# RWKV chunk loop of a four-layer encoder: right side in opposite rows, solve beside the state output on four blocks, 32x32 completion between 64x64 products

## The chip, the cores and the metric

The kernel runs on one core of one Trainium2 chip. The metric is the device time of one execution in microseconds. Three executions of the kernel before took 1472.31, 1472.85 and 1475.32 us (median 1472.85).

## The reference, cut to what matters

The model is an encoder of four layers on one sequence of 512 tokens of width 1024, all in float32: an RWKV-7 mixer, windowed attention, an mLSTM mixer, and a second RWKV-7 mixer. The change touches the two RWKV-7 mixers. In the reference their core is a scan over tokens with a 64x64 state for each of 16 heads:

```python
def step(S, inp):
    r_t, w_t, k_t, v_t, kk_t, b_t = inp
    sa = jnp.einsum('bhvk,bhk->bhv', S, -kk_t)
    S = S * w_t[:, :, None, :] + sa[..., None] * b_t[:, :, None, :] + v_t[..., None] * k_t[:, :, None, :]
    return S, jnp.einsum('bhvk,bhk->bhv', S, r_t)
```

The kernel works in 8 chunks of 64 tokens. Inside a chunk the values `sa` of all tokens depend on each other through a strictly triangular 64x64 matrix A for each head, so that they come from a triangular solve: `sa = -(I + A)^-1 * right side`. The inverse is put together from 32x32 parts: both diagonal 32x32 blocks are inverted for all chunks and heads at once before the loop, and the off-diagonal block is the product inverse * A-block * inverse with a minus sign. That last step is called the completion here.

## The kernel before, in words

The program is written by hand: each engine has its own instruction list, and semaphores (`wait_ge`, `then_inc`) order them. `rw_mix` is one RWKV layer up to the heads' outputs. Its projections fill TensorE with 128x128 by 512 products; then comes the chunk loop over `c` in 0..7. The 16 heads are kept as 8 pairs `p`, the even head of a pair in partitions 0 to 63 (`LO`), the odd one in 64 to 127 (`HI`). All matrices of a head are 64x64, so that a product of one head fills one of the four 64x64 blocks of the array. Which block is set by the rows where the operands lie and by the rows of the bank that it writes.

All products of the layer but the projections go through `mm` at line 848, so that the profile shows them under L848; the transposes of B and K are L959. A float32 product appears as two MATMUL and two LDWEIGHTS records; a transpose as one.

TensorE's list in chunk c, in order:

1. `complete_and_begin(c)`: 16 products for the completion (lower left part of the inverse, out to banks 2 and 3), and between them 16 products that begin the right side (A_k * V, out to banks 4 and 5). The completion products use LO->LO and HI->HI, the others the two crossed blocks.
2. `right_side_state(c)`: 16 products KK * S, added in banks 4 and 5, on LO->LO and HI->HI.
3. `turn_values(c+1)`: 16 products with 128 rows and 64 columns, to banks 0 and 1.
4. `products_r(c+1)`: 32 products on all four blocks, to banks 2 and 3.
5. `solve(c)`: 16 products, completed inverse times right side, on LO->LO and HI->HI, to banks 6 and 7.
6. `x(c+1)`: 16 products of 64x64, A times the placed 32x32 inverses, to banks 0 and 1.
7. `outputs(c)`: 16 products S * L (the state's output), then for each half of the pairs 8 products with 128 rows for the output and 8 with 128 rows for the state.
8. `turn_bk(c+1)`: 8 transposes of 128x128, to banks 0 and 1.

ScalarE (ACT) in chunk c: `read_rhs` (L599, two), `values(c+1)` (L592 and L593, two each), `read_sa` (L606, four), `read_y` (L612, two), `keep_bkt(c+1)` (L557 to L559, six), and `place_inverse(c+2)` (L581, four copies that put the 32x32 inverses into a zeroed 64x64 tile, 128 columns wide with its transpose). VectorE (DVE): `mask_r(c+1)` (L679, two), `mask_x(c+1)` (L746, two), `advance(c)` (L758 and L762), `complete_u(c+1)` (L752, two), `place_transpose(c+2)` (L732, four). GpSimd squares the outputs (L512) beside them. SyncE's list has two things in the loop: the reload of h after chunk 3, and the next weights, which wait for the last `us_ready`, since the placed inverses lie in the weights' slots.

What the change touches: the constants at lines 360 to 380, the views `tu`, `xs`, `us`, `x_bank` (419 to 445), SyncE's wait (488), GpSimd's memset (507), `place_inverse` (571, with its calls 628 to 642), `place_transpose`, `mask_x`, `complete_u` (724 to 753), VectorE's loop (829 to 844), and TensorE's functions from line 914 to 1083.

Of the kernel before, what the change touches and what calls it, by code (L numbers as in the profile page):

```python
# [9 lines left out]
ALU = mybir.AluOpType  # L10
# [3 lines left out]
P = 128  # L14
T = 512
D = 1024
KT = D // P
NT = T // P
C = 64
# [343 lines left out]
A_US = A_XS + 512  # L363
A_S = A_US + 512
# [15 lines left out]
SIDES = ((0, LO), (1, HI))  # L380

# [10 lines left out]
def rw_mix(m, prm, w2a2, reset_src, n0, spill):  # L392
# [29 lines left out]
    gmask, xmask = m.view(A_CONST + C_GMASK, P), m.view(A_CONST + C_XMASK, C)  # L422
# [6 lines left out]
    tu = [m.view(m.slot(n0 + 29 + c), KT, P) for c in range(NC)]  # L429
    z = [m.view(A_Z + 1024 * (c % 2), NH, C) for c in range(NC)]  # L430
    xs, us = m.view(A_XS, KT, C), m.view(A_US, KT, C)
# [4 lines left out]
    quarter = lambda bank: bank[:, 0:256].rearrange("p (k c) -> p k c", c=C)  # L436
    blocks = lambda bank: bank[:, :].rearrange("p (k c) -> p k c", c=P)
# [11 lines left out]
    for j in range(KT):  # L449
# [16 lines left out]
    gathered, step, t_turned, tu_cleared, t_placed, u_placed = (m.sem(n) for n in (  # L466
        "gathered", "inverse_step", "t_turned", "tu_cleared", "t_placed", "u_placed"))
# [7 lines left out]
    with nc.Block() as block:  # L475
        @block.sync
        def _(sp):
# [10 lines left out]
            sp.wait_ge(us_ready.handle, us_ready.at(2 * NC))  # L488
# [4 lines left out]
        def _(pool):  # L493
# [10 lines left out]
            for c in range(BC):  # L504

                pool.wait_ge(tile_done.handle, tile_done.at(place["g", BC + c] + 1))
                nc.gpsimd.memset(tu[c], 0.0).then_inc(tu_cleared.handle, 1)
# [7 lines left out]
        def _(act):  # L515
# [55 lines left out]
            def place_inverse(c):  # L571

                if c == 0:
                    act.wait_ge(t_turned.handle, t_turned.at(1))
                if c < BC:
                    act.wait_ge(tu_cleared.handle, tu_cleared.at(c + 1))
                else:
                    act.wait_ge(us_ready.handle, us_ready.at(2 * (c - BC + 1)))
                for g in range(4):
                    rows, at = slice(Q * g, Q * g + Q), Q * (g % 2)  # L580
                    last = nc.scalar.activation(tu[c][rows, :, at:at + Q],  # L581
                                                tt[rows, c // BC, :, KT * (c % BC):KT * (c % BC) + KT]
                                                .rearrange("p c n -> p n c"), ACT.Copy)
                last.then_inc(t_placed.handle, 1)

# [42 lines left out]
            place_inverse(0)  # L628
# [3 lines left out]
            place_inverse(1)  # L632
            for c in range(NC):
# [7 lines left out]
                if c + 2 < NC:  # L641
                    place_inverse(c + 2)

        @block.vector
        def _(dve):
# [78 lines left out]
            def place_transpose(c):  # L724

                if c < BC:
                    dve.wait_ge(tu_cleared.handle, tu_cleared.at(c + 1))
                else:
# [1529 lines left out]
```

## Time and profile before

| | |
|---|---|
| median of three executions | 1472.85 us |
| the profiled execution | 1473.26 us |
| its span in the trace | 1471.2 us |
| mean granted TensorE clock over the span | 0.98 of full |
| TensorE busy (matrix products) | 1356.5 us, 92% |
| VectorE busy | 719.3 us, 49% |
| ScalarE busy | 440.6 us, 30% |
| records under L848 | 6720, 187.6 us |

The span is the time from the first to the last instruction of the one profiled execution; the 2.1 us between it and the time of that execution lie around it. Busy times of TensorE are the union of its overlapping records: a stretch can be full of records and yet pass few of them, so that counts and start times say more than the busy share. In the timelines of the trace a row merges neighbouring instructions of one line and engine; its first number is the start in us from the span's start, the second the time covered, `x192` the number of records, and the bracket is the idle time ahead of the row and what ended it.

### The profile page before, as it was taken

To read this page: it belongs to the slowest core of one execution; us is meant where nothing else is said; L and a number is where in the kernel's file an instruction comes from. 1 tells how busy PE (TensorE), PEld (TensorE's weight loads), DVE (VectorE), ACT (ScalarE), POOL (GpSimd) and SP (SyncE) were. 2 spreads that over 40 slices of the span, in tenths; PEclk is the share of its full clock that TensorE was granted. 3 is DMA by queue.
4 is the path that set the end of the run, shared out by engine and by line. 5 is a ranking of instruction groups with operands and counts; after the bars stand their busy time and mean duration, and the time that the engine had idled before them with its cause. 6 is when DMAs were issued, how large, how long until landed. Compare 5 with 4: busy or idle time off the path is not lost. (4 is left out here: it accounts for less than half of the span.)

```text
span 1471.2 us, 23885 instructions
## 1 busy us (share of the span) xinstructions
PE 1356.5 (92%) x10291; PEld 713.6 (49%) x10291; DVE 719.3 (49%) x1388; ACT 440.6 (30%) x964; POOL 90.7 (6%) x82
## 2 busy tenths in 40 slices
PE   5999999988798999889899989898999999988897
PEld 3444444487544444464444446544444444478633
DVE  5784656855643002261344023434684755955552
ACT  1114243277401011460112052501114253177501
POOL 0000240100000000000000000000000241000000
PEclk9999999999999999999999989998999999999989
DMA  6222222001400222101222221113222222101211
GB/s 208 72 72 56 61 70 62 25 4 61 176 0 1 73 84 72 58 2 57 74 71 72 72 56 29 57 57 113 80 72 57 72 59 69 32 4 61 75 58 57
DMA packets 111184, 92.47 MB, mean 63 GB/s; under 512 B 5020, under 2 KB 99524, under 8 KB 110568
## 3 DMA queue, kind: packets, MB, share of 16 engines
q1 hardware_dynamic: 110376, 88.81, 19.9%
q8 instruction: 82, 1.34, 0.4%
q10 hardware_dynamic: 704, 2.13, 0.4%
q14 instruction: 22, 0.18, 0.0%
HBM read 84.64 MB, written 6.29 MB: 62 GB/s over the span
## 5 line engine op out<-in xcount | busy, mean ns | idle before, releaser
L893 PE MATMUL bank<-arena 128*128 128x512 f32 x960 | 420.1, 594 | 1.5 <-ACT arena L541 1.5
L893 PEld LDWEIGHTS bank<-arena 128*128 128x128 f32 x960 | 180.6, 190 | 224.9 <-issue 219.1
L848 PE MATMUL bank<-arena 64*64 64x64 f32 (+2 forms) x6720 | 187.6, 225 | 29.8 <-ACT arena L599 8.9
L848 PEld LDWEIGHTS bank<-arena 64*64 64x64 f32 (+1 forms) x6720 | 164.5, 135 | 66.0 <-issue 37.5
L1215 PE MATMUL bank<-arena 128*128 128x512 f32 x256 | 116.9, 618 | 4.7 <-DVE arena L1180 4.7
L159 ACT ACTIVATE arena<-arena 128x1024 f32<-128x1024 f32 x20 | 21.1, 1055 | 244.6 <-DVE arena L1186 133.4
L1215 PEld LDWEIGHTS bank<-arena 128*128 128x128 f32 x256 | 50.2, 198 | 71.8 <-issue 64.7
L1679 PE MATMUL bank<-arena 128*128 128x512 f32 x160 | 71.0, 605 | 1.6 <-PEq L301 1.6
L653 DVE SCALAR_TENSOR_TENSOR arena<-arena 128x512 f32<-128x512 f32 x96 | 72.2, 802 | 0.0
L495 POOL MEMSET arena<- 128x8 f32 x2 | 0.2, 113 | 932.9 <-DVE arena L808 932.9
L1311 PE MATMUL bank<-arena 128*128 128x512 f32 x128 | 55.2, 593 | 1.6 <-PEq L1124 1.6
L2088 PE MATMUL bank<-arena 128*128 128x512 f32 x128 | 55.8, 593 | 0.9 <-DVE arena L2132 0.9
L310 PE MATMUL bank<-arena 128*128 128x512 f32 x128 | 55.2, 593 | 1.0 <-PEq L1427 1.0
L565 ACT ACTIVATE arena<-arena 32x256 f32<-32x256 f32 x64 | 41.4, 647 | 47.0 <-DVE arena L673 46.5
L1342 PE MATMUL bank<-arena 128*128 128x512 f32 x128 | 55.2, 591 | 0.0
L1660 PE MATMUL bank<-arena 128*128 128x512 f32 x128 | 55.1, 592 | 0.0
L786 DVE RECIPROCAL arena<-arena 128x512 f32<-128x512 f32 x16 | 53.6, 3352 | 0.5
L541 ACT ACTIVATE arena<-bank 128x512 f32<-128x512 f32 x32 | 19.0, 595 | 115.1 <-PE bank L893 115.1
L1679 PEld LDWEIGHTS bank<-arena 128*128 128x128 f32 x160 | 30.8, 194 | 41.5 <-issue 41.5
L539 ACT ACTIVATE arena<-bank 128x512 f32<-128x512 f32 x16 | 9.6, 597 | 122.6 <-PE bank L893 75.2
L1876 PE MATMUL bank<-arena 128*128 128x512 f32 x96 | 42.9, 592 | 0.0
L1392 DVE TENSOR_TENSOR arena<-arena 128x160 f32<-128x160 f32 x16 | 4.1, 320 | 78.9 <-ACT arena L1369 78.7
(233 smaller groups left out, 1652.3 us busy)
## 6 DMA issues: line engine op xcount, KB each, us to landing
arena<-in_rw_w_in SPq DMA_DIRECT2D x66, 512.0 KB, 4.1
arena<-in_ml_w_in SPq DMA_DIRECT2D x24, 512.0 KB, 3.8
arena<-in_sw_w_in SPq DMA_DIRECT2D x20, 512.0 KB, 3.7
arena<-in_rw_w_out SPq DMA_DIRECT2D x16, 512.0 KB, 7.1
spill<-arena SPq DMA_DIRECT2D x2, 2048.0 KB, 8.4
arena<-spill SPq DMA_DIRECT2D x2, 2048.0 KB, 8.5
arena<-in_sw_w_out SPq DMA_DIRECT2D x8, 512.0 KB, 3.7
arena<-in_ml_w_out SPq DMA_DIRECT2D x8, 512.0 KB, 3.7
```

The costliest lines, as they stand in the source:

```text
L310: return nc.tensor.matmul(m.bank[2 * a + half][:, :], Y[:, k, a * P:(a + 1) * P], slot[:, k % 2, :], start=k == 0, stop=k == KT - 1)
L653: nc.vector.scalar_tensor_tensor(out=mix_at[g][:, k, :], in0=dx[:, k, :], scalar=col(mu_at[g], k), in1=xt[:, k, 1:T + 1], op0=ALU.mult, op ...
L786: link(nc.vector.reciprocal(rt, rt))
L848: mm = lambda out, a, b, start=True, stop=True: nc.tensor.matmul(out, a, b, start=start, stop=stop, skip_group_check=True)
L893: last = nc.tensor.matmul(bank[:, :], slot[:, k, :], mix_at[what][:, k, :], start=k == 0, stop=k == KT - 1)
L1215: return nc.tensor.matmul(nc_out[:, :], Y[:, k, a * P:(a + 1) * P], W[:, k, 512 * half:512 * half + 512], start=k == 0, stop=k == KT - 1)
L1311: last = nc.tensor.matmul(m.bank[n][:, :], xt[:, k, 1 + (n // 2) * P:1 + (n // 2 + 1) * P], slot[:, 512 * (n % 2):512 * (n % 2) + 512], st ...
L1342: last = nc.tensor.matmul(m.bank[4 + j % 4][:, :], slot[:, k, :], xt[:, k, 1:T + 1], start=k == 0, stop=k == KT - 1)
L1660: last = nc.tensor.matmul(tile_bank(n + i)[:, :], xt[:, c, 1 + (i // 2) * P:1 + (i // 2 + 1) * P], slot[:, 512 * (i % 2):512 * (i % 2) + 5 ...
L1679: last = nc.tensor.matmul(bank[:, :], slot[:, c, :], xt[:, c, 1:T + 1], start=c == 0, stop=c == KT - 1)
L1876: last = nc.tensor.matmul(z_bank(i)[:, :], m.view(m.slot(n0 + i), KT, P)[:, c, :], xt[:, c, 1:T + 1], start=c == 0, stop=c == KT - 1)
L2088: return nc.tensor.matmul(out_bank(a, half)[:, :], Y[:, k, a * P:(a + 1) * P], slot[:, k % 2, :], start=k == 0, stop=k == KT - 1)
```

## The change

The completion's products become 32x32 with the needed rows and columns alone. `x(c, p)` multiplies the off-diagonal 32x32 block of A with the inverse where that lies after the inversion (`tt`, a moving operand whose neighbouring elements are 32 apart), from rows 0:32 and 64:96 (`EARLIER`) to rows 32:64 and 96:128 (`LATER`) of bank 2. `xu(c, p)` multiplies that with `uu`, from the rows `LATER` to the rows `EARLIER` of the other half of bank 3. The copies of `place_inverse` go; `place_transpose` writes 64x64 tiles `u[c]` with the two heads' rows exchanged, and `complete_u` writes the missing 32x32 part into them with a factor of -1. The right side is formed in the opposite rows: `begun` takes LO->LO and HI->HI, KK * S and the solve take the crossed blocks. Between the products of `right_side_state(c)` stand those of `x(c + 1, p)`; between the products that begin the right side those of `xu(c, p)`; between the products of the solve those of the state's output. `products_r(c + 1)` moves behind the solve. All waits follow. Constants, semaphore names and the addresses of S and rhs change with it.

```diff
+EARLIER, LATER = (slice(0, 32), slice(64, 96)), (slice(32, 64), slice(96, 128))
+CROSSED = ((LO, HI), (HI, LO))
...
-    tu = [m.view(m.slot(n0 + 29 + c), KT, P) for c in range(NC)]
+    u = [m.view(m.slot(n0 + 29 + c // 2) + KT * C * (c % 2), KT, C) for c in range(NC)]
+    of_chunk = lambda inv, c, p: inv[:, c // BC, :, KT * (c % BC) + p]
...
-    x_bank = lambda c, g: m.bank[g if c else 2 + g]
+    x_bank, xu_bank = m.bank[2], m.bank[3]
...
-            sp.wait_ge(us_ready.handle, us_ready.at(2 * NC))
+            sp.wait_ge(sa_done.handle, sa_done.at(2 * NC))
             m.load_weights(sp, n0 + 33 + SLOTS)
...
-                if c + 2 < NC:
-                    place_inverse(c + 2)
...
 def place_transpose(c):
-                if c < BC:
-                    dve.wait_ge(tu_cleared.handle, tu_cleared.at(c + 1))
-                else:
-                    dve.wait_ge(us_ready.handle, us_ready.at(2 * (c - BC + 1)))
+                dve.wait_ge(u_cleared.handle, u_cleared.at(c // 2 + 1))
                 for g in range(4):
-                    rows, at = slice(Q * g, Q * g + Q), C + Q * (g % 2)
-                    last = nc.vector.tensor_copy(tu[c][rows, :, at:at + Q],
-                                                 uu[rows, c // BC, :, KT * (c % BC):KT * (c % BC) + KT]
+                    rows, to, at = slice(Q * g, Q * g + Q), slice(Q * (g ^ 2), Q * (g ^ 2) + Q), Q * (g % 2)
+                    last = nc.vector.tensor_copy(u[c][to, :, at:at + Q], uu[rows, c // BC, :, KT * (c % BC):KT * (c % BC) + KT]
...
-            def mask_x(c):
-                for g in range(2):
-                    dve.wait_ge(x_done.handle, x_done.at(2 * c + g + 1))
-                    nc.vector.tensor_tensor(xs[:, pairs[g], :], quarter(x_bank(c, g)), wide(xmask, 4), ALU.mult)\
-                        .then_inc(xs_ready.handle, 1)
+            def keep_x(c):
+                dve.wait_ge(x_done.handle, x_done.at(c + 1))
+                for rows in LATER:
+                    last = nc.vector.tensor_copy(xs[rows], small(x_bank)[rows])
+                last.then_inc(xs_ready.handle, 1)
 
             def complete_u(c):
-                for g in range(2):
-                    dve.wait_ge(xu_done.handle, xu_done.at(2 * c + g + 1))
-                    nc.vector.tensor_tensor(us[:, pairs[g], :], tu[c][:, pairs[g], C:P], quarter(m.bank[2 + g]), ALU.subtract)\
-                        .then_inc(us_ready.handle, 1)
+                dve.wait_ge(xu_done.handle, xu_done.at(c + 1))
+                for rows in EARLIER:
+                    last = nc.vector.tensor_scalar(u[c][rows, :, Q:C], small(xu_bank)[rows], -1.0, None, ALU.mult)
+                last.then_inc(us_ready.handle, 1)
...
             for c in range(NC):
                 if c + 1 < NC:
+                    keep_x(c + 1)
+                    place_transpose(c + 1)
                     mask_r(c + 1)
-                    mask_x(c + 1)
                 advance(c)
                 if c + 1 < NC:
                     complete_u(c + 1)
-                if c + 2 < NC:
-                    place_transpose(c + 2)
...
+            def x_begin(c):
+                if c == 0:
+                    pe.wait_ge(ga_evac.handle, ga_evac.at(2 * NC))
+                    pe.wait_ge(t_turned.handle, t_turned.at(1))
+                else:
+                    pe.wait_ge(gr_evac.handle, gr_evac.at(2 * given["r"]))
+                given["x"] = c + 1
+
+            def x(c, p):
+                for par in range(2):
+                    last = mm(x_bank[LATER[par], Q * p:Q * p + Q], ga[c][EARLIER[par], 2 * p + par, Q:C],
+                              of_chunk(tt, c, p)[EARLIER[par]])
...
+            def xu(c, p):
+                for par in range(2):
+                    last = mm(xu_bank[EARLIER[1 - par], Q * p:Q * p + Q], xs[LATER[par], p, :], of_chunk(uu, c, p)[LATER[par]])
...
             def complete_and_begin(c):
...
                     for k in range(4):
                         p = 4 * g + k
-                        for par, rows in SIDES:
-                            completed = mm(m.bank[2 + g][rows, C * k:C * k + C], xs[rows, p, :], tu[c][rows, p, C:P])
-                        for par, (rows, others) in enumerate(((LO, HI), (HI, LO))):
+                        xu(c, p)
+                        for par, (rows, others) in enumerate(CROSSED):
                             h = 2 * p + par
-                            begun = mm(m.bank[4 + g][rows, C * k:C * k + C], ga[c][others, h, :], z[c][others, h, :], k == 0, False)
+                            begun = mm(m.bank[4 + g][others, C * k:C * k + C], ga[c][others, h, :], z[c][others, h, :], k == 0, False)
...
             def right_side_state(c):
+                if c + 1 < NC:
+                    x_begin(c + 1)
...
-                        for par, rows in SIDES:
-                            last = mm(m.bank[4 + g][rows, C * k:C * k + C], KK[rows, p, span(c)], S[rows, p, :], False, k == 3)
+                        for rows, others in CROSSED:
+                            last = mm(m.bank[4 + g][others, C * k:C * k + C], KK[rows, p, span(c)], S[rows, p, :], False, k == 3)
+                        if c + 1 < NC:
+                            x(c + 1, p)
                     last.then_inc(rhs_done.handle, 1)
 
             def solve(c):
+                pe.wait_ge(us_ready.handle, us_ready.at(c + 1))
+                pe.wait_ge(u_placed.handle, u_placed.at(c + 1))
...
-                        for par, rows in SIDES:
-                            last = mm(m.bank[6 + g][rows, C * k:C * k + C], us[rows, p, :], rhs[rows, p, :])
-                    last.then_inc(sa_done.handle, 1)
+                        for rows, others in CROSSED:
+                            solved = mm(m.bank[6 + g][rows, C * k:C * k + C], u[c][others, p, :], rhs[others, p, :])
+                        for rows, others in CROSSED:
+                            mm(m.bank[4 + g][rows, C * k:C * k + C], S[rows, p, :], L[rows, p, span(c)], k == 0, False)
+                    solved.then_inc(sa_done.handle, 1)
...
                 right_side_state(c)
                 if c + 1 < NC:
                     turn_values(c + 1)
-                    products_r(c + 1)
                 solve(c)
                 if c + 1 < NC:
-                    x(c + 1)
+                    products_r(c + 1)
                 outputs(c)
```

## Rows read from the trace of the kernel before

**Rows 1.** Page: busy time, share of the span, number of instructions.
```profile
span 1471.2 us, 23885 instructions
PE 1356.5 (92%) x10291; PEld 713.6 (49%) x10291; DVE 719.3 (49%) x1388; ACT 440.6 (30%) x964; POOL 90.7 (6%) x82
```
**Rows 2.** Busy time by stretch: seven chunks and the last, both layers.
```profile
core 0: us, PE busy (x) PEld busy (x) DVE busy (x) ACT busy (x) POOL busy (x), PEclk, DMA share, GB/s
294.57:379.57 85.00, 74.39 (x2520) 68.80 (x2520) 45.33 (x98) 63.86 (x153) 7.15 (x7) 1.00 0.08 29
379.57:387.81 8.24, 6.18 (x225) 5.83 (x224) 3.38 (x7) 4.90 (x15) 1.17 (x2) 1.00 0.68 244
...
1293.87:1378.57 84.70, 74.97 (x2522) 69.10 (x2522) 45.38 (x98) 63.88 (x153) 7.17 (x7) 1.00 0.09 29
```
**Rows 3.** Groups by line, 294.57 to 379.57: busy us, mean ns, idle before.
```profile
L848 PE MATMUL bank<-arena 64*64 64x64 f32 (+1 forms) x2464 | 67.7, 221 | 11.3 <-ACT arena L593 4.7 <-ACT arena L599 4.2 <-issue 1.1
L581 ACT ACTIVATE arena<-arena 32x256 f32<-32x256 f32 x28 | 18.2, 650 | 0.4
L732 DVE COPY arena<-arena 32x256 f32<-32x256 f32 x28 | 10.6, 378 | 0.3
```
**Rows 4.** Timeline of chunk 6, to the start of chunk 7.
```profile
367.51 4.41 PE L848 MATMUL bank<-arena 64*64 64x64 f32 x192
...
369.15 0.38 ACT L559 ACTIVATE arena<-bank 64x256 f32<-64x256 f32 x1
369.56 2.64 ACT L581 ACTIVATE arena<-arena 32x256 f32<-32x256 f32 x4
369.64 2.13 PEld L848 LDWEIGHTS bank<-arena 128*64 128x64 f32 x96 [0.19 <-issue]
371.97 1.29 DVE L679 TENSOR_TENSOR arena<-bank,arena 128x512 f32<-128x512 f32 x2 [1.36 <-PE bank L848]
372.22 0.66 ACT L599 ACTIVATE arena<-bank 128x256 f32<-128x256 f32 x2
...
372.66 1.15 PE L848 MATMUL bank<-arena 64*64 64x64 f32 x32 [0.74 <-ACT arena L599]
372.91 0.38 ACT L592 ACTIVATE arena<-bank 64x256 f32<-64x256 f32 x1
...
374.37 1.55 ACT L606 ACTIVATE arena<-bank 64x256 f32<-64x256 f32 x4
...
374.52 4.10 PE L848 MATMUL bank<-arena 64*64 64x64 f32 x128 [0.71 <-ACT arena L593]
375.25 0.89 DVE L746 TENSOR_TENSOR arena<-bank,arena 128x256 f32<-128x256 f32 x2 [1.99 <-PE bank L848]
377.27 0.38 ACT L612 ACTIVATE arena<-bank 128x256 f32<-128x256 f32 x1 [1.34 <-PE bank L848]
...
378.55 1.09 PE L959 MATMUL bank<-arena 128*128 128x128 f32 x8
...
379.24 0.38 ACT L557 ACTIVATE arena<-bank 128x256 f32<-128x256 f32 x1 [0.66 <-PE bank L959]
```
**Rows 5.** TensorE's and ScalarE's timeline of chunk 7, the last.
```profile
379.57 2.08 PE L848 MATMUL bank<-arena 64*64 64x64 f32 x96
...
382.06 4.10 PE L848 MATMUL bank<-arena 64*64 64x64 f32 x128 [0.41 <-ACT arena L599]
```
**Rows 6.** Timeline from the last projection to the first chunk.
```profile
283.71 7.13 PE L893 MATMUL bank<-arena 128*128 128x512 f32 x16
...
284.24 0.19 PEld L893 LDWEIGHTS bank<-arena 128*128 128x128 f32 x1 [0.24 <-issue]
284.67 0.19 PEld L893 LDWEIGHTS bank<-arena 128*128 128x128 f32 x1 [0.24 <-issue]
...
290.77 2.08 PE L848 MATMUL bank<-arena 64*64 64x64 f32 x96
```
**Rows 7.** TensorE's timeline: the chunk with the issue gap, first layer.
```profile
330.01 4.41 PE L848 MATMUL bank<-arena 64*64 64x64 f32 x192
...
339.07 3.40 PE L848 MATMUL bank<-arena 64*64 64x64 f32 x104 [1.14 <-issue]
342.39 1.10 PE L959 MATMUL bank<-arena 128*128 128x128 f32 x8
```

More of the change, by code:

```diff
@@ L436, in rw_mix @@
     quarter = lambda bank: bank[:, 0:256].rearrange("p (k c) -> p k c", c=C)
+    small = lambda bank: bank[:, 0:256].rearrange("p (k c) -> p k c", c=Q)
     blocks = lambda bank: bank[:, :].rearrange("p (k c) -> p k c", c=P)
@@ L465, in rw_mix @@
     s_cleared, scaled_rk = m.sem("s_cleared"), m.sem("scaled_rk")
-    gathered, step, t_turned, tu_cleared, t_placed, u_placed = (m.sem(n) for n in (
-        "gathered", "inverse_step", "t_turned", "tu_cleared", "t_placed", "u_placed"))
+    gathered, step, t_turned, u_cleared, u_placed = (m.sem(n) for n in (
+        "gathered", "inverse_step", "t_turned", "u_cleared", "u_placed"))
     rhs_begun, v_done, v_evac, x_done, xs_ready, xu_done, us_ready, s_added =  (m.sem(n) for n in (
@@ L569, in gather @@
                     last.then_inc(gathered.handle, 1)
-            def place_inverse(c):
-                if c == 0:
-                    act.wait_ge(t_turned.handle, t_turned.at(1))
-                if c < BC:
-                    act.wait_ge(tu_cleared.handle, tu_cleared.at(c + 1))
-                else:
[L578 to L584, printed above, removed]
             def values(c):
@@ L831, in _ @@
                 gate(j)
-            mask_x(0)
+            keep_x(0)
             mask_r(0)
             complete_u(0)
-            place_transpose(1)
             for c in range(NC):
                 if c + 1 < NC:
+                    keep_x(c + 1)
+                    place_transpose(c + 1)
                     mask_r(c + 1)
-                    mask_x(c + 1)
                 advance(c)
@@ L915, in banks_01_read @@
                 pe.wait_ge(v_evac.handle, v_evac.at(2 * given["values"]))
[L916 removed]
                 pe.wait_ge(bkt_evac.handle, bkt_evac.at(2 * given["turned"]))
             def banks_23_read():
[L920 removed]
+                pe.wait_ge(xs_ready.handle, xs_ready.at(given["x"]))
+                pe.wait_ge(us_ready.handle, us_ready.at(given["xu"]))
                 pe.wait_ge(gr_evac.handle, gr_evac.at(2 * given["r"]))
@@ L970, in turn_values @@
                 given["values"] = c + 1
-            def x(c):
-                if c > 0:
-                    banks_01_read()
-                else:
-                    pe.wait_ge(ga_evac.handle, ga_evac.at(2 * NC))
-                pe.wait_ge(t_placed.handle, t_placed.at(c + 1))
-                for g in range(2):
-                    for k in range(4):
-                        p = 4 * g + k
-                        for par, rows in SIDES:
-                            last = mm(x_bank(c, g)[rows, C * k:C * k + C], ga[c][rows, 2 * p + par, :], tu[c][rows, p, 0:C])
-                    last.then_inc(x_done.handle, 1)
-                given["x"] = c + 1
+            def x_begin(c):
+                if c == 0:
+                    pe.wait_ge(ga_evac.handle, ga_evac.at(2 * NC))
+                    pe.wait_ge(t_turned.handle, t_turned.at(1))
+                else:
+                    pe.wait_ge(gr_evac.handle, gr_evac.at(2 * given["r"]))
[4 more added lines that the diff above has]
+                              of_chunk(tt, c, p)[EARLIER[par]])
+                if p == KT - 1:
+                    last.then_inc(x_done.handle, 1)
+            def xu(c, p):
+                for par in range(2):
+                    last = mm(xu_bank[EARLIER[1 - par], Q * p:Q * p + Q], xs[LATER[par], p, :], of_chunk(uu, c, p)[LATER[par]])
+                if p == KT - 1:
+                    last.then_inc(xu_done.handle, 1)
             def complete_and_begin(c):
                 banks_23_read()
-                pe.wait_ge(u_placed.handle, u_placed.at(c + 1))
+                given["xu"] = c + 1
                 if c == 0:
@@ L1065, in _ @@
             project(len(tiles) - 1)
-            x(0)
+            x_begin(0)
+            for p in range(KT):
+                x(0, p)
             products_r(0)
@@ L1089, in rw_mix @@
                  (gr_evac, 2 * NC), (bkt_done, 2 * NC), (bkt_evac, 2 * NC), (gathered, 1), (step, steps[0]), (t_turned, 1),
-                 (tu_cleared, BC), (s_cleared, 1), (scaled_rk, NC), (t_placed, NC), (u_placed, NC)):
+                 (u_cleared, BC), (s_cleared, 1), (scaled_rk, NC), (x_done, NC), (xs_ready, NC), (xu_done, NC), (us_ready, NC), (u_placed, NC)):
         s.base += n
-    for s in (rhs_begun, v_done, v_evac, x_done, xs_ready, xu_done, us_ready, s_added, rhs_done, rhs_evac, sa_done, sa_evac, y_done,
+    for s in (rhs_begun, v_done, v_evac, s_added, rhs_done, rhs_evac, sa_done, sa_evac, y_done,
               y_evac, s_done, s_ready):
```

28 lines of the change are left out of this document (6 added, 22 removed).

## The prediction

> **What bounds the kernel now.** I read the page's busy times first, then the chunk loops by stretch, then one chunk in the timeline. TensorE is busy 92% of the span, the others half of it or less [rows 1]. The change touches only the two chunk loops: seven chunks take 85.0 us in the first layer and 84.7 in the second, and the last chunk about 8 more [rows 2]. So it can move about 185 us of 1473; the rest is the projections' 128x128 products.
>
> A plain chunk lasts 12.05 us (379.57, where the next begins, less 367.51) [rows 4, 5]. The reader should see there that TensorE isn't full. The solve (372.66) and x (374.52) each start after 0.7 us of idle time, ended by ScalarE [rows 4]. ScalarE is busy 63.9 of 85 us [rows 2], and 18.2 of these are the L581 copies of `place_inverse` [rows 3]: they run from 369.56 to 372.20, and right behind them, at 372.22, comes the L599 copy for which the solve waits [rows 4].
>
> **TensorE's prices.** Products come in steps. The solve's 16 products are 32 records over 1.15 us; less the last record's own 0.22 [rows 3] and a start of 0.05 that is 0.058 us for each step of two records [rows 4]. In chunk 7 `complete_and_begin` (64 records, four blocks) and `right_side_state` (32 records, two blocks) take 2.08 us together [rows 5]. Less 0.22 these are 1.86 us, 32 steps of 0.058: 16 for the two-block products, so 16 for the others. Four blocks pass four records in the step in which two blocks pass two. Hence products on idle blocks are free, and that is what the change uses.
>
> Against this stands the price of another block size. From 374.52 to 378.55 there are 128 records, 64 steps or 3.73 us, but 4.03 pass: 0.30 over, for the start and for two changes, from 64 to 128 rows in the middle and to the transposes' 128x128 at the end [rows 4]. That is 0.15 us each. The projection's 16 records at 0.43 (284.24 to 284.67) would take 6.88 us; from 283.71 to 290.77 it is 7.06, 0.18 over for the changes around it, with larger weights [rows 6]. I read 0.09 of the 0.15 as the array running empty and 0.05 as the first weights, which nothing hides any more (twice that with 128 columns, hence the 0.18). Every change of size in these rows pays. The Trainium skill says the same in "TensorEngine Tiling (Array Packing)", Key Properties: changing the tiling mode, not just the tile, drains TensorE. By that rule 32x32 between 64x64 pays at each turn; by block independence alone (rival 1) it pays nothing. No row here has 32x32 products, and all changes in the rows are between blocks that overlap, so the trace doesn't decide it.
>
> **The change, part by part.** Mechanism of the forecast: a drain at each change between 32x32 and 64x64.
>
> - *Interleaved completion.* In `complete_and_begin` each pair p has two 32x32 products and two 64x64 products; in `right_side_state` two 64x64 and two 32x32. A batch of two 64x64 products is 2 steps (0.117) plus a change (0.145): 0.262 us. A batch of two 32x32 products has half the columns: 0.058 + 0.09 + 0.025 for half the weights = 0.175. Eight pairs: 8 x 0.437 = 3.50 us a stage, instead of 0.93. The second stage begins with the size with which the first ends: 7.00 - 0.15 = 6.85 us instead of 1.86, +4.99. Bounds for the 32x32 batch: 0.14 (weights hidden) to 0.30 (no shorter than 64x64, and the operand with neighbours 32 apart read slower: the ScalarE copy of it took 650 ns for 256 elements, the plain L592 copy 380 [rows 3, 4]).
> - *x gone as a stage.* Its 32 records (0.93 us) and the wait ahead of it (0.71 plus about 0.2 until products pass) go: -1.85.
> - *State output beside the solve* on the other two blocks: -0.93.
> - *products_r behind the solve.* The time stays (0.93). It covered ScalarE's work ahead of the solve; now only `turn_values` does. ScalarE without L581 is free at 369.53; rhs is done with the right side at 6.85 + 0.25, the two L599 end at 7.7 us into the chunk, `turn_values` at 7.93: the solve doesn't wait. That wait of 0.7 (0.9 until products pass) goes, and so does the 0.3 us wait of `turn_values` for the last L559 copy, which the longer first stages cover.
> - *Next limit.* `outputs` waits for `read_sa`, which stands behind four value copies: values begin at 7.4 + 0.45, four copies of 0.39 to 9.4, two copies of `read_sa` to 10.15, while TensorE reaches `outputs` at 6.85 + 1.08 + 1.96 = 9.9 to 10.05. I count 0.1.
> - *VectorE* does less: `keep_x` reads 32 of 64 rows twice, about the two L746; the four L732 (1.5 us) stand behind `keep_x` in a stretch where it idled 1.4 to 2 us [rows 4]. Its longest new chain, the two L679 of 1.29 us behind r, ends at about 11.5, before the next chunk's first product needs the banks. Cost 0; if it were late, `complete_and_begin` would wait for it.
> - *SyncE*: the four weight loads wait for the last `sa_done`, some 4 us later than the last `us_ready` came. They serve a stage after the whole of `rw_gate_out`. 0. The u tiles' memsets are the same four on GpSimd. 0.
>
> The chunk by addition: 6.85 + values 1.08 + solve and r 1.96 (32 steps and a change) + outputs 2.02 (32 steps and a change) + transposes 1.02 (378.55 to 379.57) + 0.1 = 13.0 us against 12.05 [rows 4, 5]. One gap of 1.14 us stands in the first layer's loop inside products, with no releaser ("issue") [rows 7]; such gaps (1.3 and 1.05 us by layer, the 85.0 and 84.7 less 7 x 12.05 and plus 0.7, by which chunk 0 is shorter) I leave in. Seven chunks: 91.0 + 1.3 = 92.3 and 92.1, +7.4 each.
>
> Last chunk: 3.50 + 0.93, the solve 0.2 later (rhs read), 1.0, then `outputs` waits for `read_sa` until 6.15, and ends at 8.1. Before it was 2.49 + 3.9 = 6.4 [rows 5]. +1.7. Before the loop, x(0) shrinks from 0.93 to 0.47 plus one more change: -0.3.
>
> A layer: 7.4 + 1.7 - 0.3 = +8.8; two: +17.6. The profiled execution took 1473.26 us (span 1471.2 and 2.1 around it): 1490.9, and 1490.5 from the median of 1472.85. Forecast 1491. Its own range: with the 32x32 batch at 0.30, 16 x 0.125 = 2.0 us more a chunk, +32, reached only if both bad ends hold; with 0.14, -0.55 a chunk, -9; so 1478 to 1515.
>
> **Rivals.**
>
> 1. *No drain, since the blocks are disjoint.* x lies inside LO->LO and HI->HI while KK * S takes the crossed blocks; xu lies inside the crossed ones. If the array only waits where sub-blocks overlap, both stages keep 0.93. For it: every change in the rows was between overlapping blocks. The Trainium skill, "TensorE: Matmul & The Clock Gate", Part 3, tells of 32x32 tiles that run side by side, but all of one size. Then `turn_values` still starts at 2.17 (the L559 copies end at 2.03), the solve at 3.25, r ends at 5.2, `outputs` waits for `read_sa` until 5.35 and ends at 7.4, the transposes at 8.4: 8.45 a chunk, -3.6. Seven chunks -24.5, the last -0.5, x(0) -0.3: -25.3 a layer, 1422 us. 0.22.
> 2. *Changes cost only the 0.09.* If the weights of the next size load while the array empties: 8 x (0.21 + 0.15) = 2.86 a stage, a chunk of 11.8, -1.1 a layer for seven and +1.05 for the last, -0.3: 1472. It lies next to the point where the sign turns: with changes for nothing and no overlap of sizes the chunk would be 16 x 0.175 + 6.2 = 9.0 us, 3.05 less than now, and it has 31 changes: 0.1 us for each. 0.08.
> 3. *No drain, but no overlap*: the small products add 16 steps of 0.029 a stage, 0.93 a chunk less what they cover of the ScalarE wait: 1437. 0.06.
> 4. *A drain at each pass*: every product is two records; if the passes of a batch alternate sizes, the changes double, about +4.5 us a chunk more: 1560. Against it: the records of one product are issued one after the other. 0.03.
>
> The forecast has 0.61.
>
> **How the numbers follow.** About 3 us (0.2%) can be told from no change. Faster: rival 1, rival 3 and 0.03 of rival 2, 0.31. Same: 0.04. Slower: 0.65. The likeliest case's own range is 1478 to 1515. The range for 8 in 10 has to take in both signs: half of rival 1 and above, up to nearly the end of the forecast's: 1420 to 1510.
>
> **What would show it.** In the trace after, `complete_and_begin` with `right_side_state` (128 records) takes 6.9 us if right, 1.9 by rival 1, 2.8 by rival 3, 5.6 by rival 2; LDWEIGHTS rows break up into groups of four records with idle time before each. L581 is gone, and no wait for L599 stands ahead of the solve. The solve with the state's output and r are 128 records in 1.9 us without a wait between. `outputs` waits 0.1 us for L606. The prediction is wrong if the 32x32 records pass in the steps of the 64x64 ones; its size is wrong if a pair takes far from 0.44 us.

## The result, and the profile after

The changed kernel takes 1547.59 us (median of 4, 1545.33 to 1548.11) against 1474.09 us (median of 4, 1472.31 to 1475.43) for the kernel before: a ratio of 1.0493 [1.0477, 1.0509], 73.5 us slower. The forecast was 1491, with 1510 as its upper end. The sign came out, and so did the cost of a change of block size; but the loss is four times the 18 us forecast, for a reason that the forecast didn't hold.

In the changed file TensorE's helper `mm` is L826, the transposes L937, `read_rhs` L587, the value copies L580 and L581, `read_sa` L594, `read_y` L600, `complete_u` L732, `keep_x` L726, `place_transpose` L713, `mask_r` L663. First the page of the kernel after, its span, busy times and granted clock in 40 slices.

```profile
span 1545.8 us, 23757 instructions
PE 1449.5 (94%) x10291; PEld 774.0 (50%) x10291; DVE 718.0 (46%) x1388; ACT 402.1 (26%) x900; POOL 90.7 (6%) x82
PEclk9999999876799999999999989998999999877899
```

As many matrix instructions as before (10291), 93 us more of busy TensorE [rows 1], and two long dips of the clock. The dips are the two chunk loops, as the busy times by stretch of the kernel after show (columns as in [rows 2]).

```profile
295.75:414.04 118.29, 118.29 (x2521) 97.89 (x2521) 44.42 (x98) 47.18 (x125) 7.15 (x7) 0.71 0.06 21
414.04:425.05 11.01, 9.18 (x225) 7.88 (x225) 3.37 (x7) 5.04 (x15) 1.17 (x2) 0.85 0.26 86
1333.88:1451.72 117.84, 116.04 (x2520) 95.72 (x2520) 44.48 (x98) 47.18 (x125) 7.15 (x7) 0.74 0.06 21
1451.72:1462.75 11.03, 9.18 (x226) 7.89 (x225) 3.38 (x7) 5.05 (x15) 1.17 (x2) 0.85 0.01 3
```

Seven chunks take 33.3 and 33.1 us more than in [rows 2], the last chunk 2.8 and 2.7 (it took 8.24 and 8.33): 71.9 of the 73.5 us lie in the loops. VectorE's time is the same, ScalarE's has fallen from 63.9 to 47.2 us. TensorE is never idle by its records in the first loop, and yet it passes no more of them than before (2521 to 2520); the granted clock over the stretch is 0.71, where it was 1.00. TensorE's timeline of the kernel after, chunks 0, 1 and 3 and the head of 4 (a row mixes all sizes, and shows the first):

```profile
295.75 15.83 PE L826 MATMUL bank<-arena 32*32 32x32 f32 x352 [0.70 <-DVE arena L663]
...
312.53 15.22 PE L826 MATMUL bank<-arena 32*32 32x32 f32 x352
327.68 1.09 PE L937 MATMUL bank<-arena 128*128 128x128 f32 x8
...
345.77 16.11 PE L826 MATMUL bank<-arena 32*32 32x32 f32 x352
361.82 1.09 PE L937 MATMUL bank<-arena 128*128 128x128 f32 x8
362.84 16.11 PE L826 MATMUL bank<-arena 32*32 32x32 f32 x352
```

A chunk from 345.77 to 362.84 is 17.07 us; it was 12.05 [rows 4, 5]. Chunks 2 to 6 all repeat this pattern, without a wait inside. What happens in chunk 1 on the other engines (the same kernel):

```profile
316.18 0.85 DVE L732 TENSOR_SCALAR arena<-bank 32x256 f32<-32x256 f32 x2 [3.23 <-PE bank L826]
...
317.87 0.39 ACT L587 ACTIVATE arena<-bank 128x256 f32<-128x256 f32 x1 [3.31 <-PE bank L826]
...
320.27 0.38 ACT L587 ACTIVATE arena<-bank 128x256 f32<-128x256 f32 x1 [2.01 <-PE bank L826]
```

The last completion product is out by 3.65 us after the chunk's head (316.18 less 312.53), the right side by 7.74 us (forecast: 7.1). And the granted clock by stretch, of the kernel after:

```profile
312.53:318.49 5.96, 5.96 (x107) 4.21 (x106) 1.25 (x3) 2.34 (x7) 0.13 (x1) 1.00 0.01 3
318.49:325.32 6.83, 6.83 (x170) 6.17 (x172) 2.32 (x6) 3.41 (x9) 0.00 (x0) 0.50 0.01 4
...
342.40:349.23 6.83, 6.83 (x160) 5.54 (x152) 3.24 (x6) 3.05 (x8) 1.04 (x1) 1.00 0.01 2
349.23:359.47 10.24, 10.24 (x217) 8.61 (x217) 3.16 (x8) 3.79 (x10) 0.00 (x0) 0.50 0.40 139
```

The clock goes between 1.00 and 0.50 (2.4 and 1.2 GHz): from the third chunk on 10.24 us at half and 6.83 at full, together one chunk. By the starts of the single records, a pair (two 32x32 and two 64x64 products, a batch each) takes 0.474 us at the full clock, 0.262 of it the 64x64 batch and 0.212 the 32x32 one; at half clock it takes 0.653 (0.408 and 0.245).

### The profile page after: what moved, and what is told of

The parts are those of the page before. It is cut to its first block and busy times, and to the rows that moved or that the text cites. A ratio compares the mean times of both kernels' runs of the same rounds, so it can differ in the third digit from the quotient of the medians.

```text
span 1545.8 us, 23757 instructions
## 1 busy us (share of the span) xinstructions
PE 1449.5 (94%) x10291; PEld 774.0 (50%) x10291; DVE 718.0 (46%) x1388; ACT 402.1 (26%) x900; POOL 90.7 (6%) x82
## 5 line engine op out<-in xcount | busy, mean ns | idle before, releaser
L871 PEld LDWEIGHTS bank<-arena 128*128 128x128 f32 x960 | 180.6, 190 | 224.9 <-issue 219.1
L826 PE MATMUL bank<-arena 64*64 64x64 f32 (+3 forms) x6720 | 278.7, 262 | 10.8 <-POOL arena L505 4.5
L826 PEld LDWEIGHTS bank<-arena 64*64 64x64 f32 (+2 forms) x6720 | 224.3, 162 | 78.4 <-issue 33.7
L1199 PEld LDWEIGHTS bank<-arena 128*128 128x128 f32 x256 | 50.0, 198 | 70.5 <-issue 64.2
L1663 PEld LDWEIGHTS bank<-arena 128*128 128x128 f32 x160 | 30.9, 194 | 41.6 <-issue 41.6
L544 ACT ACTIVATE arena<-bank 128x512 f32<-128x512 f32 x32 | 19.0, 595 | 115.2 <-PE bank L871 115.2
L1295 PEld LDWEIGHTS bank<-arena 128*128 128x128 f32 x128 | 25.0, 196 | 33.2 <-issue 33.2
```

The source lines that it names most:

```text
L826: mm = lambda out, a, b, start=True, stop=True: nc.tensor.matmul(out, a, b, start=start, stop=stop, skip_group_check=True)
L871: last = nc.tensor.matmul(bank[:, :], slot[:, k, :], mix_at[what][:, k, :], start=k == 0, stop=k == KT - 1)
L1199: return nc.tensor.matmul(nc_out[:, :], Y[:, k, a * P:(a + 1) * P], W[:, k, 512 * half:512 * half + 512], start=k == 0, stop=k == KT - 1)
L1295: last = nc.tensor.matmul(m.bank[n][:, :], xt[:, k, 1 + (n // 2) * P:1 + (n // 2 + 1) * P], slot[:, 512 * (n % 2):512 * (n % 2) + 512], st ...
L1663: last = nc.tensor.matmul(bank[:, :], slot[:, c, :], xt[:, c, 1:T + 1], start=c == 0, stop=c == KT - 1)
```

## The experiments

All ratios are against the kernel before, measured beside it on the same chip.

**e1_all64.** All small products become 64x64 ones in the same places; the small results are other numbers.

```diff
-                    last = mm(x_bank[LATER[par], Q * p:Q * p + Q], ga[c][EARLIER[par], 2 * p + par, Q:C],
-                              of_chunk(tt, c, p)[EARLIER[par]])
+                    last = mm(x_bank[rows, C * p:C * p + C], ga[c][rows, 2 * p + par, :], ga[c][rows, 2 * p + par, :])
...
-                    last = mm(xu_bank[EARLIER[1 - par], Q * p:Q * p + Q], xs[LATER[par], p, :], of_chunk(uu, c, p)[LATER[par]])
+                    last = mm(xu_bank[others, C * p:C * p + C], ga[c][rows, 2 * p + par, :], ga[c][rows, 2 * p + par, :])
```

> The changed kernel with every 32x32 product of the completion put as a 64x64 product on the same idle blocks, at the same places, with other operands (rows of A times A, so the completed inverse is not the right one and the output isn't the reference's). Theory (each change of block size empties the array, and the clock falls because of it): both interleaved stages take 0.93 us, a chunk about 8.5 us, the clock stays at its full level in the loop, 1420 to 1430 us. Rival 1 (the loss is in the new order and its waits, as products_r behind the solve or read_sa ahead of outputs): slower than 1474. Rival 2 (four blocks at once bring the clock down): the granted clock in the loop is 0.5 in some stretches here too.

Measured: 1464.36 us, ratio 0.9925 [0.991, 0.994]. With the same number of products in the same order, 83 us go when one size is kept, and with them nearly all of the half clock (0.98 over the first loop). e2 below keeps the 32x32 products, and there the half clock goes too but for a stretch behind a long stall, so the many changes of size cause the loss. But the time is 34 us above the upper end of what was expected: the chunk is 11.63 us in the mean of seven, not the 8.5 to which the steps add up. TensorE's timeline of e1_all64:

```profile
307.99 2.97 PE L826 MATMUL bank<-arena 64*64 64x64 f32 x127 [0.68 <-issue]
312.02 3.12 PE L826 MATMUL bank<-arena 64*64 64x64 f32 x127 [1.05 <-issue]
...
337.54 4.00 PE L826 MATMUL bank<-arena 64*64 64x64 f32 x96 [3.66 <-issue]
```

The engine stops after every 127 or so MATMUL records, with as many weight loads beside them, and waits for nothing that the profile shows. This is what "issue" stands for in the rows, and an issue gap here. e8 to e11 follow this up.

**e2_stretches, e3_groups4, e4_groups2.** The same products, with fewer changes of size: all small products of a stage in one stretch, in groups of four pairs, or of two. e4 for the completion; the other stage in the same way:

```diff
-                        xu(c, p)
+                        if k % 2 == 0:
+                            for i in range(2):
+                                xu(c, p + i)
```

> The changed kernel with the 32x32 products not between the others but in one stretch a stage: all sixteen xu ahead of the products that begin the right side, all sixteen x behind those of KK*S. Nothing else differs. Theory: 4 changes a chunk instead of 31; a stage takes 0.93 + 0.9 + 0.3 us, a chunk 10.3 us at full clock, 1445 to 1455 us. Rival (32x32 products with operands whose neighbours are 32 apart are slow in themselves): the x and xu stretches take over 2 us each and the time stays above 1500.

> The changed kernel, interleaved by four pairs (eight 32x32 products, then eight 64x64) instead of by one: 7 or 8 changes a chunk instead of 31. Theory: 0.15 us each over the stretches' kernel: a chunk 10.7 us, 1450 to 1460 us, the clock full or nearly so. Rival (the products, not the changes, cost): as slow as the changed kernel.

> The changed kernel, interleaved by two pairs: 15 changes a chunk. Theory: a chunk 11.7 us at full clock, 1467 to 1475 us; if the clock falls in it as in the changed kernel, up to 1500. The price of a change from the three doses should be 0.15 us while the clock is full. Rival: no difference to the changed kernel, 1547.

| kernel | changes in the two stages | the two stages, us | undisturbed chunk, us | median, us | ratio |
|---|---|---|---|---|---|
| after | 31 | 7.33 | none at full clock | 1547.59 | 1.0493 [1.0477, 1.0509] |
| e4_groups2 | 15 | 5.28 | 11.42 | 1486.85 | 1.0084 [1.0057, 1.0111] |
| e3_groups4 | 7 | 4.34 | 10.48 | 1466.79 | 0.9948 [0.9933, 0.9963] |
| e2_stretches | 3 | 3.93 | 10.08 | 1470.56 | 0.9971 [0.996, 0.9983] |

The second column counts the changes between the sizes and the one at the stages' end; all versions have the one at their head beside them. The third and fourth are at the full clock and without an issue gap. For the kernel after, the 7.33 is added up from its batches at full clock: 16 at 0.212, 14 at 0.262 and the double one between the stages, 0.275. An undisturbed chunk of e2_stretches, e3_groups4 and e4_groups2, in this order, the last with its two stages and with a stretch at half clock:

```profile
1357.59:1367.67 10.08, 10.08 (x362) 9.46 (x361) 6.02 (x14) 6.74 (x19) 0.92 (x1) 1.00 0.03 6
```
```profile
1353.15:1363.63 10.48, 10.48 (x361) 9.55 (x360) 6.01 (x14) 6.74 (x19) 0.91 (x1) 1.00 0.02 5
```
```profile
321.29:332.71 11.42, 11.42 (x361) 9.85 (x360) 6.04 (x14) 6.74 (x19) 0.91 (x1) 1.00 0.01 3
...
321.29:326.57 5.28, 5.28 (x130) 4.08 (x129) 0.83 (x2) 2.55 (x8) 0.00 (x0) 1.00 0.01 3
...
297.90:304.70 6.80, 6.80 (x144) 5.87 (x142) 3.17 (x8) 2.23 (x6) 0.00 (x0) 0.50 0.01 2
```

In the two stages four changes cost 0.41 us, eight more 0.94 and sixteen more 2.05: 0.10, 0.12 and 0.13 us each. At the full clock a chunk of the kernel after would so take 11.42 + 2.05 = 13.5 us, near the 13.0 forecast, and not 17.07. The rest appears with the half clock. In e4 it shows now and then (the last row above is one of five such stretches, 6.8 to 13.7 us long, three of them with no long gap before); in e3 and e2 only behind the long stall told of under e5. So the price isn't linear in the changes: at 31 a chunk the clock is at half for most of the time. An undisturbed chunk is 0.2 to 0.3 us shorter than expected in all three, but the medians of e2 and e3 are 16 and 7 us above the ranges expected, and e2, with the fewer changes, isn't faster than e3: issue gaps, as in e1, take what the steps give back.

**e7_filled.** Is it that half of the array's blocks stand idle in the mixed stages? 30 more 64x64 products a chunk are put on the blocks that the 64x64 batches leave free.

```diff
+                            if p < KT - 1:
+                                mm(m.bank[3][rows, 256 + C * k:256 + C * k + C], ga[c][others, h, :], z[c][others, h, :])
...
+                        for rows, others in CROSSED:
+                            mm(m.bank[2][rows, 256 + C * k:256 + C * k + C], KK[rows, p, span(c)], S[rows, p, :])
```

> The changed kernel, interleaved pair by pair with its 31 changes a chunk, plus 30 extra 64x64 products a chunk on the two blocks that stand idle while the two 64x64 products of a batch run; their results are never read. Theory (the clock falls because so little of the array is at work in these stretches, not because of the changes as such): the extra products ride along, the clock stays full for more of the loop, and the time falls from 1547 although there is more work. Rival (the changes or the short runs themselves bring the clock down): the same granted clock in the loop, 10 of 17 us at half, and 1547 or above.

Measured: 1548.54 us, ratio 1.0494 [1.0465, 1.0524], the time of the kernel after. Four chunks of e7_filled:

```profile
326.52:394.83 68.31, 68.31 (x1682) 56.77 (x1681) 25.61 (x57) 27.34 (x73) 4.16 (x5) 0.73 0.10 34
```

and the same four of the kernel after:

```profile
328.70:396.97 68.27, 68.27 (x1441) 56.57 (x1441) 25.61 (x57) 27.38 (x73) 4.16 (x5) 0.70 0.09 33
```

240 more MATMUL records pass in the same time, but with a little more of it at the full clock. By the starts of the records a filled 64x64 batch takes 0.275 us at full clock, 0.262 without: 0.2 us a chunk for 30 products, so that products on idle blocks are nearly free here too, as the prediction held of [rows 5]. Filling the blocks hardly brings the clock back: the rival of this experiment's theory held.

**e6_stretches_contiguous.** e2 with the inverse read with its neighbours side by side (the values are those of other elements).

```diff
-    of_chunk = lambda inv, c, p: inv[:, c // BC, :, KT * (c % BC) + p]
+    of_chunk = lambda inv, c, p: inv[:, c // BC, KT * (c % BC) + p, :]
```

> The kernel with 32x32 products in stretches, with the moving operand of x and xu taken as 32 neighbouring elements instead of 32 elements 32 apart (other values: the output isn't the reference's). A step of 32x32 products took 0.056 us with the spread operand where half of 0.058 was expected. If the spread is what holds them, the step falls to about 0.03 us; if weights or issue set the step, it stays 0.056, and the time stays at 1470.

Measured: 1467.23 us, ratio 0.9941 [0.9919, 0.9962], against 0.9971 of e2. The stretch of x(0) and `products_r(0)`, first in e2_stretches, then in e6_stretches_contiguous:

```profile
292.12 2.17 PE L826 MATMUL bank<-arena 32*32 32x32 f32 x96
```
```profile
290.40 1.78 PE L826 MATMUL bank<-arena 32*32 32x32 f32 x96
```

The stretch, with 16 steps of x(0), is 0.39 us shorter. By the starts of the records a step of 32x32 products falls from 0.057 to 0.032 us, and the time from the last of them to the first 64x64 product from 0.166 to 0.128. With its neighbours 32 elements apart, a product of 32 columns costs as much as one of 64.

**e5_together.** Both kinds of small products in one stretch at the chunk's head, where x(c + 1) and xu(c) take different blocks.

```diff
+                if c + 1 < NC:
+                    x_begin(c + 1)
+                for p in range(KT):
+                    if c + 1 < NC:
+                        x(c + 1, p)
+                    xu(c, p)
```

> Correct version: the x of chunk c+1 stand beside the xu of chunk c, all 32x32 on four different places, in one stretch at the head of the chunk, between the transposes and the products that begin the right side. 2 changes to and from 32x32 a chunk, and four blocks of work in the 32x32 stretch. Theory A (TensorE is the bound, steps and changes add up): 9.1 us a chunk, 1430 us. Theory B (TensorE's instructions are the bound: the runs so far show gaps without a releaser after every 128 matmul records, and 16 KB packets of the instruction queue about 3.8 us apart, so that the 720 LDWEIGHTS and MATMUL instructions of a chunk and its waits, 2.9 packets, need 11.1 us): 11.2 to 11.6 us a chunk, 1462 to 1470 us, however well the steps are packed.

Measured: 1464.32 us, ratio 0.993 [0.9902, 0.9957]. TensorE's timeline of e5_together:

```profile
294.55 8.36 PE L826 MATMUL bank<-arena 32*32 32x32 f32 x352 [0.70 <-DVE arena L663]
...
303.86 5.21 PE L826 MATMUL bank<-arena 32*32 32x32 f32 x217
309.64 3.12 PE L826 MATMUL bank<-arena 64*64 64x64 f32 x128 [0.57 <-issue]
...
328.87 2.71 PE L826 MATMUL bank<-arena 128*64 128x64 f32 x127 [0.90 <-issue]
335.40 4.04 PE L826 MATMUL bank<-arena 64*64 64x64 f32 x97 [3.81 <-issue]
```

Chunk 0 passes in 9.31 us (294.55 to 303.86), without a gap; the mean of seven is 10.90. From chunk 1 on issue gaps come in all but one chunk, one of them 3.81 us. The time is as theory B has it, the mean chunk a little shorter. Why the best versions gain 10 us, and not the 40 and more of theory A, is the question of the next four.

**e9_together_fewer and e10_together_more.** e5 without the 16 products S * L in each chunk, and e5 with 16 products more, on blocks that are idle, in seven of eight chunks. In steps of the array both are worth next to nothing.

```diff
-                        for rows, others in CROSSED:
-                            mm(m.bank[4 + g][rows, C * k:C * k + C], S[rows, p, :], L[rows, p, span(c)], k == 0, False)
```
```diff
+                            if c >= 1:
+                                mm(m.bank[6 + g][rows, 256 + C * k:256 + C * k + C], KK[rows, p, span(c)], S[rows, p, :])
```

> The version with x and xu in one stretch, without the sixteen products S*L of a chunk, which ride on the two blocks that the solve leaves idle and so take no step of their own; the output isn't the reference's. Theory B (dense stretches are held by the supply of instructions, 256 to a 16 KB packet, packets not closer than some 3.5 us): 64 instructions fewer a chunk are a quarter of a packet, 0.9 us a chunk, so 1464 falls to about 1450. Theory A (steps of TensorE are the bound, gaps have another cause): no change, 1464.

> The same version with sixteen extra products a chunk (seven chunks of eight), on the two blocks that KK*S leaves idle, into unused columns of banks 6 and 7; they take no step of their own. Theory B: a quarter of a packet more a chunk, up to 0.9 us, so 1464 rises to 1470 to 1477; less if they fall into a loose stretch. Theory A: no change, 1464.

Measured: e9 1448.82 us, ratio 0.9826 [0.9812, 0.9841]; e10 1477.58 us, ratio 1.0024 [1.0012, 1.0036]. Against e5 that is -15.5 us for 1024 instructions fewer (256 products, two loads and two passes each) and +13.3 us for 896 more: 15 ns for each instruction, both ways, though TensorE has room for them. Both times are as theory B has them (1477.58 at the end of its range). Against e11 below, measured on the same chip as these two, it is -14.9 and +13.8 us, 15 ns again. TensorE's timeline of e10_together_more, where the gaps have grown:

```profile
307.43 2.92 PE L826 MATMUL bank<-arena 64*64 64x64 f32 x126 [0.35 <-issue]
311.64 2.64 PE L826 MATMUL bank<-arena 64*64 64x64 f32 x128 [1.29 <-issue]
315.70 1.38 PE L826 MATMUL bank<-arena 128*64 128x64 f32 x39 [1.42 <-issue]
```

What comes at this pace shows in the DMA queues. e5_together, 340.62 to 370.86 (packets, MB, share of 16 engines):

```profile
q8 instruction: 9, 0.15, 2.0%
```

Nine packets of 16 KB in 30.24 us, one each 3.4 us, and in the timeline a gap after about 128 MATMUL records, 256 instructions with their loads. 256 x 15 ns is 3.8 us. So TensorE's instructions themselves arrive at about this rate, and a loop that passes more than 256 of them in that time waits for them. It isn't that an instruction takes 15 ns to issue: between two gaps e10 passes 128 records and as many loads in 2.64 us (the second row above), 10 ns each. What sets the rate of the packets wasn't looked into.

**e8_before_no_copies.** The kernel before without the L581 copies but for one element (so its inverse isn't placed): does the old loop have that limit near?

```diff
-                for g in range(4):
-                    rows, at = slice(Q * g, Q * g + Q), Q * (g % 2)
-                    last = nc.scalar.activation(tu[c][rows, :, at:at + Q],
...
+                nc.scalar.activation(tu[c][0:Q, 0, 0:1], tt[0:Q, c // BC, 0, 0:1], ACT.Copy).then_inc(t_placed.handle, 1)
```

> The kernel before, with the four copies of a chunk that place the inverse (L581, 2.6 us of ScalarE a chunk) left out but for one element, so that the output isn't the reference's. The prediction's reading: the solve waits 0.7 us for L599 only because ScalarE is still at these copies. If so the wait goes and a chunk takes 11.1 to 11.4 us, 1460 to 1463 us. If the instructions set the pace at about 11.1 us a chunk, the same wait goes but gaps without a releaser take part of its place, 1464 to 1470 us.

Measured: 1467.26 us, ratio 0.9943 [0.992, 0.9965]. The mean chunk is 11.41 us. TensorE's timeline of e8_before_no_copies (`mm` is L843 there):

```profile
310.29 4.44 PE L843 MATMUL bank<-arena 64*64 64x64 f32 x138 [0.65 <-issue]
...
336.53 4.93 PE L843 MATMUL bank<-arena 64*64 64x64 f32 x104 [3.38 <-issue]
```

Ahead of the solve and of x nothing is waited for any more, and issue gaps stand in its place, as the second reading of the expectation has it: the mean chunk lost 0.7 us (85.0/7 = 12.14 before), where the two waits had been worth 1.4 and more [rows 4]. A chunk without such a gap (342.41 to 352.57) takes 10.16 us. A chunk has some 740 instructions on TensorE (720 in records, and an estimate of 20 for its waits), 11.1 us at 15 ns. The kernel before, at 12.05, was within 1 us of this limit. Its gap of 1.14 us [rows 7] isn't the limit alone: it lies beside the reload of h, issued at 332.14, and no instruction packet came between 329.4 and 336.7. But its second loop has four shorter gaps, 0.20 to 0.56 us, three of them far from the reload (issued there at 1332.03).

**e11_together_slices.** The 3.81 us gap of e5 lies beside the reload of h. The queues of e5_together, 327.9 to 336.4:

```profile
q1 hardware_dynamic: 144, 2.10, 67.1%
q8 instruction: 1, 0.02, 0.7%
```

One packet of instructions in 8.5 us, while 2 MB come in. The second layer has the same reload, and a gap of 3.77 us beside it. e11 is e5 with the reload in four parts, in four chunks one after the other.

```diff
-            sp.dma_start(m.view(A_H, 4096), spill[0]).then_inc(reloaded.handle, 16)
+            for i in range(4):
+                sp.wait_ge(rhs_done.handle, rhs_done.at(2 * (BC + i)))
+                sp.dma_start(m.view(A_H + 1024 * i, 1024), spill[0][:, 1024 * i:1024 * i + 1024]).then_inc(reloaded.handle, 16)
```

> Correct version: as e5, with the reload of h (2 MB at once after chunk 3) cut into four transfers of 512 KB, one in each of chunks 4 to 7. In e5 an instruction packet that should come some 3.5 us after the last came 6.9 us after it, while the reload ran, TensorE stood still for 3.8 us and its clock was at half after it. If the reload holds back the packet, the 3.8 us go and smaller ones come in four places: 3 to 8 us less in all, 1456 to 1461 us. If the stall has another cause it stays at the same chunk: 1464.

Measured: 1463.74 us, ratio 0.9925 [0.9911, 0.9938], no different from e5. The timeline of e11_together_slices (`mm` is L827):

```profile
333.82 2.75 PE L827 MATMUL bank<-arena 64*64 64x64 f32 x97 [1.89 <-issue]
...
346.27 3.98 PE L827 MATMUL bank<-arena 64*64 64x64 f32 x78 [2.59 <-issue]
...
359.52 2.87 PE L827 MATMUL bank<-arena 128*64 128x64 f32 x59 [1.88 <-issue]
```

The stall broke up with the reload, so the reload does hold the instructions back: four gaps of 1.88 to 2.59 us, in chunks 3 to 6 (the fourth is 1.91 us), stand in place of the long one. But the gain that was expected didn't come. The two loops of e5_together, then of e11_together_slices:

```profile
294.55:370.86 76.31, 67.55 (x2520) 62.78 (x2520) 44.44 (x98) 46.31 (x125) 7.14 (x7) 0.98 0.09 32
1287.08:1368.25 81.17, 68.47 (x2521) 62.93 (x2521) 44.81 (x98) 46.32 (x125) 7.15 (x7) 0.98 0.09 30
```
```profile
294.29:375.20 80.91, 69.77 (x2520) 64.64 (x2520) 44.14 (x98) 46.42 (x125) 7.16 (x7) 0.96 0.10 30
1293.58:1369.47 75.89, 66.99 (x2521) 61.80 (x2521) 44.79 (x98) 46.42 (x125) 7.16 (x7) 1.00 0.11 32
```

The first loop is 4.6 us longer, the second, where no gap is over 1.41 us, 5.3 shorter: in sum the same.

## Why the prediction was right and wrong

- *A change of size costs time, disjoint blocks or not*: right, and the core of the forecast. e1 (30 changes a chunk fewer, -83 us) and the series e2 to e4 show it. The 64x64 batch was put at 0.262 us and takes 0.262. Rivals 1 and 3 (no drain) fall with it, and rival 4: the two passes of a batch stand together in the records, one change a batch. Rival 2 gave 5.6 us for the two stages, which take 7.33. How a change splits into the array running empty (put at 0.09) and the first weights (0.05) no run shows. The Trainium skill says in "TensorEngine Tiling (Array Packing)", Key Properties, that a change of tiling mode drains TensorE. The runs agree, for blocks that don't overlap too, and put 0.10 to 0.13 us on a change.
- *The 32x32 batch at 0.175*: mis-sized, it takes 0.212 at the full clock. Over some 15 batches a chunk that is 0.55 us, 8 us in both loops. Most of the 0.037 is the spread operand by e6: the first step of a stretch and the last with the change behind it take 0.053 + 0.128 = 0.181 us there. It wasn't run interleaved pair by pair. The forecast had it among its bounds, and took the low side.
- *The sum of the chunk, 13.0 us*: right for what it holds. With 0.55 for the batches it is 13.55; the runs give 13.5 at the full clock, 7.33 us of it for the two stages that were put at 6.85.
- *The clock*: this is the step that failed. Every term went by the granted 1.00 of [rows 2], and nothing in the working asked whether it would stay. The 14 chunks took 236.1 us; at 13.5 each they would have taken 189, and 2 are an issue gap in the second loop. That leaves some 45 us, about 60% of the 73.5, for the 10.24 of 17.07 us at 0.50. This share is a difference, not a run: none had 31 changes and the full clock throughout. The 13.5, against 12.14 in the mean before, makes 19 us, and the last chunks 5.5.
- *ScalarE and its waits*: as forecast. L581 of before is gone, its busy time fell by 16.7 us, no wait stands ahead of the solve, and `outputs` doesn't wait either. The gain is in the sum.
- *The last chunk +1.7*: measured 2.8 and 2.7, with the clock at 0.85 in it. *x(0) -0.3*: it took 2.17 us with `products_r(0)`, where 2.08 stood before [rows 6]: with the spread operand the small step isn't shorter.
- *Rival 1's 1422*: wrong for a second reason. Without drains (e1) the steps sum to 8.5 us a chunk, but the instructions come for one in about 11.1. None of the versions here with as many of them reached it; the best (e1 and e11) are at 0.9925 of before. The range reached down to 1420 on that account.

*Left open*: what in the mixed stages brings the clock down. The runs show that it goes with the number of changes (31: 10.24 of 17.07 us; 15: five stretches; 7 and 3: only behind the reload's stall) and that more work on the idle blocks hardly helps (0.73 over four chunks, where 0.70 stood). Whether it is the change itself or the time in which the array passes nothing isn't shown. A loop that idles as much between products without changing size wasn't tried.

## What to carry to other kernels

Keep products of one block size in long stretches, even where the blocks are disjoint: each change costs 0.10 to 0.13 us by itself, and many of them in a row can cost the clock, which was the larger part here. Before counting what a removed wait gives back in a loop of small products, count its instructions on TensorE, times 15 ns: issue gaps without a releaser are a hint that this limit is near, though one alone can come from a large transfer beside it. e5_together is the version to keep, 0.993 of before; the next gain lies in fewer instructions (e9, which leaves out products that the result needs, shows 0.983), not in a better order.

## What the runs showed of the hardware that was not expected

- The granted clock fell to half in stretches that are busy by every record (118.29 of 118.29 us at 0.71). By the busy share alone nothing would be seen; the clock column shows it.
- In the dense loops TensorE's instructions come in packets of 16 KB, every 3.4 us in e5 (nine in 30.24 us), for about 256 instructions each (15 ns an instruction, by adding and by taking away). Beside a transfer of 2 MB one packet came in 8.5 us, and TensorE stood still for 3.81.
- A 32-column moving operand with neighbours 32 elements apart takes 0.057 us a step of 32x32 products, 0.032 with neighbours side by side.
- 64x64 products on blocks that the running batch leaves idle cost nearly nothing in the array, also between changes of size (e7: 0.013 us a batch); what they cost in a dense loop is their place in the supply of instructions (e10: 13 us for 224 of them).
